# A weighted sum of 128 weight pieces moved from VectorE to TensorE's column tiles, and a norm's 1/rms moved behind the products

## The chip, the cores and the metric

One core of one Trainium2 chip runs the whole program. The metric is the device time of one execution in microseconds (us); lower is better. The engines are called as in the profile: PE (TensorE; PEld is its weight loading), DVE (VectorE), ACT (ScalarE), POOL (GpSimd) and SP, whose queue issues nearly all transfers.

## What is computed

Three blocks follow each other on 256 tokens of width 2048, all in float32.

1. The first block has two layers. Each layer is an RMS norm, one wide input projection, three kinds of attention (A with 6 heads, B with 6, C with 4), a gate on each head's output, and an output projection that is added to x:

```
h = _rms_norm(x, norm_g[l])
proj = jnp.einsum('bsd,dn->bsn', h, w_in[l])
a_out = a_out.reshape(Bsz, S, A_DIM) * jax.nn.silu(a_gate)
x = x + jnp.einsum('bsm,md->bsd', mixed, w_out[l])
```

2. The second block is one layer of banded attention, modulated by rows that are computed from a conditioning vector c: `silu(c) @ w_ada + b_ada`, eight rows of 2048 numbers (six for this and the next block, two for the final norm). They depend on nothing in the first block. The product is a matrix of 2048 x 16384 numbers with one vector, 128 MB that are read once.
3. The third block routes each token to two of 32 experts and reads all experts' weights.

`_rms_norm(x, g)` is `x * rsqrt(mean(x*x) + eps) * g`. The factor rsqrt(...) is one number for each token, so it commutes with a product over the features: (r x g) W = r ((x g) W).

## The kernel before

**Pieces.** The weights of the first and second block come in pieces of 128 x 2048 numbers, 1 MB each: 73 pieces for each layer of the first block and 52 for the second block. A piece of the kinds "tok" and "out" holds 4 tiles of 128 features by 512 columns and gives rows of tokens; a piece of the kind "feat" holds 16 tiles of 128 by 128 and gives rows of features. The product is made exact with three TensorE passes: ACT copies a piece into a rounded head (`split_head`, L736), DVE subtracts to get the tail (`split_tail`, L1141), and PE multiplies head by head, head by tail and tail by head (`three`, L925 to L927): 24 matmuls over 512 columns for a tok or out piece, 48 over 256 columns for a feat piece. ACT and DVE split two pieces ahead of PE (`AHEAD`); three split pieces fit at a time.

**The modulation pieces** (`w_ada`, 128 of them) share the ring of five 1 MB buffers (`raw`) with the weights. The stream alternates: weight piece g+2, then modulation piece a, and so on; 16 out of 18 weight pieces have one beside them (`ada_after`). DVE handles such a piece in the step "ada": the piece times one number of silu(c) for each partition, added to a sum of 128 x 2048 (L1217 for the first, L1221 for the other 15 of a row). After 16 pieces PE sums over the partitions with a matrix of ones in four matmuls with 32 stationary columns each (step "ada_sum", L1109), ACT copies the result, and PE transposes it (step "ada_turn", L1117).

**Order.** Every engine walks the same list of steps (`layer_schedule`): a piece, and behind it the steps due there ("score", "turn", "value", "gate", "subnorm", "ada", ...). "turn" is the transposition of the softmax's probabilities (L1085), "value" the product with the values (L1094, L1096), both for one head. Each engine runs its own part in that order, and semaphores connect them. The layer begins with a step "norm": ACT squares x, POOL takes the power -1/2 of the mean, DVE makes a diagonal matrix of 1/rms (L1166), PE multiplies all of x with it (transposed and scaled at once, 32 matmuls, L939), and ACT and DVE write the gained result and its head and tail. Only then does the first piece begin: it waits for the last tail.

**PSUM.** There are eight banks of 128 x 512. In the first block, products rotate over banks 0 to 3, scores use 4 and 5, "turn", "subnorm", "ada_sum" and "ada_turn" share 6, "value", "forget" and "cumsum" share 7 (`psum_plan`). A step that writes a bank first waits until the bank's last content has been read (`bank_for`). The second block has a plan of its own: both heads of a "turn" pair use bank 6, one after the other (L1805, read by ACT L1687).

**The third block** starts after the second. It reads 384 MB of expert weights through a ring of its own; its first transfers are issued when the block starts.

Of the kernel before, what the change touches and what calls it, by code (L numbers as in the profile page):

```python
# [27 lines left out]
P = 128  # L28
# [22 lines left out]
for _name, _n in (("norm_g", 16), ("qn_g", 4), ("kvn_g", 2), ("b_forget", 6), ("lam", 256),  # L51
                  ("subln_g", 1), ("lam_init", 1), ("one_minus", 1), ("w_f", 96)):
    PAR[_name] = (_at, _at + _n)
    _at += _n
# [3 lines left out]
class Tally:  # L58
# [6 lines left out]
    def add(self, sem, event):  # L65
        table = self.order.setdefault(sem, {})
        assert event not in table, (sem, event)
        table[event] = len(table) + 1

    def total(self, sem):  # L70
        return len(self.order.get(sem, {}))

    def at(self, sem, event, it=0, each=1):

        n = self.order[sem][event]
        if isinstance(it, int):
            return each * (it * self.total(sem) + n)
        return it * (each * self.total(sem)) + each * n

    def end(self, sem, it=0, each=1):  # L80
        n = self.total(sem)
        return each * (it + 1) * n if isinstance(it, int) else it * (each * n) + each * n
# [137 lines left out]
def first_parameters(norm_g, qn_g, kvn_g, b_forget, lams, subln_g, w_in):  # L220

    par = np.zeros((DEPTH + 1, P, N_PAR), np.float32)

    def put(name, l, a):
        par[l, :, PAR[name][0]:PAR[name][1]] = a
    for l in range(DEPTH):
# [4 lines left out]
        put("lam", l, np.concatenate([v[l] for v in lams])[None, :])  # L231
# [5 lines left out]
    return par  # L237
# [33 lines left out]
def layer_schedule():  # L271
# [12 lines left out]
    def followers(i, piece):  # L284
# [6 lines left out]
        if i == 0:  # L291
            out.append((i, ("forget",)))
        if i == 2:
# [23 lines left out]
        if piece[0] == "out" and piece[2] == 3:  # L317
            out.append((i + 1, ("squares", piece[1])))
# [20 lines left out]
    return [("norm",)] + steps  # L339


def psum_plan(steps, tally):
# [6 lines left out]
    def take(event, bank=None):  # L349
# [3 lines left out]
        where[event] = bank  # L353
        tally.add(f"full{bank}", event)
        tally.add(f"free{bank}", event)

    n_score = 0
    for s in steps:
        kind = s[0]
        if kind == "norm":  # L360
            for j in range(8):
                take(("norm", j))
# [48 lines left out]
ACT_LINKS_1 = 1  # L411
DVE_LINKS_1 = 71
# [12 lines left out]
def first_block(nc, whole, ctx, d, x, ssq_x, c0, mod):  # L425
    steps = layer_schedule()
    tally = Tally()
    bank_of = psum_plan(steps, tally)
# [9 lines left out]
    gate_no = {g: n for n, g in enumerate(gates)}  # L438

# [14 lines left out]
    for i in range(n_pieces):  # L454
        for part in range(2):
            tally.add("head_split", (i, part))
# [2141 lines left out]
```

## Time and profile before

| | |
|---|---|
| median of 3 runs | 2504.33 us (2497.93 to 2508.22) |
| profiled execution, its own time | 2505.9 us |
| its span | 2504.1 us, so 1.8 us lie around it |
| PE busy / PEld busy | 2264.2 us (90%) / 1680.4 us (67%) |
| DVE busy | 1413.3 us (56%); 282.4 us of it are the 120 instructions of L1221 |
| ACT busy | 727.6 us (29%) |
| HBM read | 757.28 MB, 304 GB/s over the span |
| first block / second / third | about 0 to 1063, 1063 to 1479, 1479 to 2504 us |

Busy time is the union of an engine's instructions. A matmul's record is longer than the step from one matmul to the next, since they are pipelined: steps are read from the differences of the start times. One float32 matmul (as in L1109, L939, L1094) leaves two records, so "x8" means four matmuls. The granted clock (PEclk) is given as a share of 2.4 GHz; 0.5 is 1.2 GHz.

### The profile page before, as it was taken

The numbers are of one execution on the slowest core, as the hardware profiler recorded it, in microseconds if no ns is written. First come the engines' busy times: TensorE is split into PE (matmuls) and PEld (weight loads), VectorE is DVE, ScalarE is ACT, GpSimd is POOL, SyncE is SP. The second block draws the span as 40 slices with busy tenths as digits, with TensorE's granted clock in tenths as the row PEclk, the third lists the DMA queues.
The fourth block names the chain that finished last, engine by engine and source line by source line (L and its number), as shares of the span: only waits on it lengthen the run. The fifth ranks groups of instructions, "written<-read, shape, count | busy, mean of one in ns | idle before, by whom it ended". The sixth has DMA issues, their size and how long they took to land. (4 is left out here: it accounts for less than half of the span.)

```text
span 2504.1 us, 37242 instructions
## 1 busy us (share of the span) xinstructions
PE 2264.2 (90%) x14757; PEld 1680.4 (67%) x14757; DVE 1413.3 (56%) x2015; ACT 727.6 (29%) x1347; POOL 40.7 (2%) x62
## 2 busy tenths in 40 slices
PE   6999999989999998979999987999888888888886
PEld 5889988778899997867788774454444444444442
DVE  3878799875787898855545535333333333333334
ACT  3443544442443544345545422000000000000001
POOL 0100000000000000030000000000000000000000
PEclk8999999998999999989999987999999999999998
DMA  5877767865877776774334434999999999999997
GB/s 215 330 305 291 276 236 269 305 270 215 348 263 291 262 262 255 290 261 141 132 126 138 143 143 185 421 422 422 422 422 422 422 422 422 422 422 422 422 422 312
DMA packets 108689, 761.83 MB, mean 304 GB/s; under 512 B 12288, under 2 KB 15520, under 8 KB 16800
## 3 DMA queue, kind: packets, MB, share of 16 engines
q1 hardware_dynamic: 108288, 759.30, 76.8%
q8 instruction: 76, 1.25, 0.2%
q10 hardware_dynamic: 288, 0.98, 0.1%
q14 instruction: 37, 0.30, 0.0%
HBM read 757.28 MB, written 2.95 MB: 304 GB/s over the span
## 5 line engine op out<-in xcount | busy, mean ns | idle before, releaser
L2263 PE MATMUL b_ps<-s_raw,s_window 128*64 128x256 f32 x4096 | 461.0, 382 | 58.7 <-DVE x_tokens L2489 39.3
L2263 PEld LDWEIGHTS b_ps<-s_raw,s_window 128*64 128x64 f32 x4096 | 295.3, 137 | 236.0 <-issue 72.6
L1141 DVE TENSOR_TENSOR s_w_tail<-s_raw,s_w_head 128x1024 fp32r<-128x1024 f32 x292 | 345.3, 1223 | 44.8 <-ACT s_w_head L736 44.7
L925 PE MATMUL b_ps<-s_h_head,s_w_head 128*128 128x256 f32 x1184 | 345.2, 292 | 0.0
L926 PE MATMUL b_ps<-s_h_tail,s_w_head 128*128 128x256 f32 x1184 | 337.9, 285 | 0.0
L927 PE MATMUL b_ps<-s_h_head,s_w_tail 128*128 128x256 f32 x1184 | 337.9, 285 | 0.0
L736 ACT ACTIVATE s_w_head<-s_raw 128x1024 fp32r<-128x1024 f32 x292 | 293.8, 1052 | 129.1 <-DMA s_raw<-in_w 76.4
L1221 DVE SCALAR_TENSOR_TENSOR s_ada_acc<-s_raw,s_c_col,s_ada_acc 128x2048 f32<-128x2048 f32 x120 | 282.4, 2354 | 0.0
L2283 PE MATMUL b_ps<-s_raw,s_diag 128*64 128x512 f32 x1024 | 238.3, 600 | 39.9 <-DMA s_raw<-in_w_down 24.6
L925 PEld LDWEIGHTS b_ps<-s_h_head,s_w_head 128*128 128x128 f32 x1184 | 230.1, 194 | 13.1 <-issue 11.0
L926 PEld LDWEIGHTS b_ps<-s_h_tail,s_w_head 128*128 128x128 f32 x1184 | 230.4, 195 | 0.2
L927 PEld LDWEIGHTS b_ps<-s_h_head,s_w_tail 128*128 128x128 f32 x1184 | 230.0, 194 | 0.0
L2171 ACT ACTIVATE s_hidden<-b_ps 128x256 f32<-128x256 f32 x32 | 12.3, 384 | 645.3 <-PE b_ps L2263 645.3
L2283 PEld LDWEIGHTS b_ps<-s_raw,s_diag 128*64 128x64 f32 x1024 | 65.9, 136 | 191.6 <-DMA s_raw<-in_w_down 84.1
L2481 DVE TENSOR_TENSOR s_y<-b_ps,s_gate_row 128x512 f32<-128x512 f32 x64 | 44.3, 692 | 238.3 <-PE b_ps L2283 238.3
L925 PE MATMUL b_ps<-s_w_head,s_h_head 128*128 128x512 f32 x416 | 168.1, 404 | 6.4 <-issue 6.4
L926 PE MATMUL b_ps<-s_w_tail,s_h_head 128*128 128x512 f32 x416 | 166.3, 400 | 0.0
L2489 DVE TENSOR_TENSOR x_tokens<-b_ps,x_tokens 128x1024 f32<-128x1024 f32 x128 | 147.8, 1217 | 32.5 <-PE b_ps L2298 32.5
L927 PE MATMUL b_ps<-s_w_head,s_h_tail 128*128 128x512 f32 x416 | 165.8, 399 | 0.0
L1840 DVE TENSOR_TENSOR s_w_tail<-s_raw,s_w_head 128x1024 fp32r<-128x1024 f32 x104 | 126.3, 1253 | 69.5 <-ACT s_w_head L1611 69.3
L1730 PE MATMUL b_ps<-s_h_head,s_w_head 128*128 128x256 f32 x416 | 121.0, 291 | 0.0
L1731 PE MATMUL b_ps<-s_h_tail,s_w_head 128*128 128x256 f32 x416 | 118.9, 286 | 0.0
(340 smaller groups left out, 3168.2 us busy)
## 6 DMA issues: line engine op xcount, KB each, us to landing
s_raw<-in_w SPq DMA_DIRECT2D x198, 1024.0 KB, 5.8
s_raw<-in_w_ada SPq DMA_DIRECT2D x128, 1024.0 KB, 5.1
s_raw<-in_w_gate SPq DMA_DIRECT2D x128, 1024.0 KB, 24.1
s_raw<-in_w_up SPq DMA_DIRECT2D x128, 1024.0 KB, 26.5
s_raw<-in_w_down SPq DMA_DIRECT2D x128, 1024.0 KB, 26.8
x_tokens<-in_x SPq DMA_DIRECT2D x1, 2048.0 KB, 7.7
s_rel<-in_rel SPq DMA_DIRECT2D x1, 2048.0 KB, 11.5
s_raw<-mod_rows SPq DMA_DIRECT2D x2, 1024.0 KB, 12.2
```

What stands on the lines that cost most here:

```text
L736: act.activation(w_head[:, g % SPLITS, cols], raw[:, ring, cols], ACT.Copy)\
L925: pe.matmul(out, head, m_head, start=first, stop=False, skip_group_check=True)
L926: pe.matmul(out, head, m_tail, start=False, stop=False, skip_group_check=True)
L927: return pe.matmul(out, tail, m_head, start=False, stop=last, skip_group_check=True)
L1141: dve.tensor_tensor(w_tail[:, g % SPLITS, cols], raw[:, slot["w", g], cols], w_head[:, g % SPLITS, cols].bitcast(F32), ALU.subtract)\
L1221: ins = dve.scalar_tensor_tensor(out=ada_acc[:, :], in0=raw[:, ring, :], scalar=c_col[:, 2, k:k + 1], in1=ada_acc[:, :], op0=ALU.mult, op1 ...
L1730: pe.matmul(out, head, m_head, start=first, stop=False, skip_group_check=True)
L1731: pe.matmul(out, head, m_tail, start=False, stop=False, skip_group_check=True)
L1840: dve.tensor_tensor(w_tail[:, i % SPLITS, cols], raw[:, i % RAW, cols], w_head[:, i % SPLITS, cols].bitcast(F32), ALU.subtract)\
L2263: ins = pe.matmul(psum[64 * h:64 * h + 64, c // 4, 0:T], window[:, 4 * (c % 4) + k, :], raw[:, c, k * 512 + h * T:k * 512 + h * T + T], st ...
L2283: ins = pe.matmul(psum[rows_n, 4 + n % 2, :], hidden_t[:, m_ % 2, 64 * (m_ // 2):64 * (m_ // 2) + 64], raw[:, 8 + m_, n * 512:(n + 1) * 51 ...
L2489: dve.tensor_tensor(xs, psum[:, bank:bank + 2, :], xs, ALU.add).then_inc(sem["x_added"], 1)
```

## The change

- Each modulation piece is multiplied and summed by PE: four matmuls with 32 equal stationary columns (the piece's column of silu(c), repeated), one for each 512 columns of the piece, written to four groups of 32 partitions of bank 7, and accumulated there over 16 pieces (L1149 in the changed kernel). The steps "ada" on DVE and "ada_sum" on PE are gone; ACT copies the bank instead.
- x is transposed without 1/rms (L967, `turn_x`), and its head and tail are made of x times the gain. The transposition of the next layer's x is spread between the last pieces of the layer and the first pieces of the next. 1/rms is applied to the outputs: as ACT's scale for tok pieces, as a DVE product with a row `rrow` for q, k and gates. DVE, not ACT, now reads q, k and gate outputs from PSUM. The gate's sigmoid is three ACT instructions (Exp, Ln, Exp) instead of one on ACT and a reciprocal on DVE.
- Bank plan of the first block: "value", "forget" and "cumsum" move from bank 7 to bank 6. "forget" and "cumsum" come 4 pieces later. Parameters of both layers are loaded at the start.
- Second block: the second head of each "turn" pair gets bank 3, and the feat pieces' banks are assigned anew.

```diff
@@ all_steps, new
+NEXT_NORM = {("out", 1, 3): [("squares", 0), ("turn_x", 0)],
+             ("out", 2, 0): [("squares", 1), ("turn_x", 1), ("split_x", 0)],
+             ("out", 2, 1): [("split_x", 1)],
+             ("out", 3, 0): [("squares", 2), ("turn_x", 2)],
+             ("out", 3, 2): [("split_x", 2)],
+             ("out", 3, 3): [("split_x", 3)]}
+
+THIS_NORM = {("tok", 0, 0): [("squares", 3), ("turn_x", 3)],
+             ("tok", 0, 1): [("split_x", 4)],
+             ("tok", 0, 2): [("x_rows",)]}
...
@@ psum_plan
-        elif kind in ("turn", "subnorm", "ada_sum", "ada_turn"):
+        elif kind == "ada" and s[1] % 16 == 0:
+            take(("ada_sum", s[1] // 16), 7)
+        elif kind in ("turn", "subnorm", "ada_turn"):
             take(s, 6)
         elif kind in ("value", "forget", "cumsum"):
-            take(s, 7)
+            take(s, 6)
...
@@ TensorE
+                if kind == "turn_x":
...
+                                ins = pe.transpose(ps[:, col:col + P], x_tiles[:, t, 4 * n + 2 * j + k, :], ident)
...
-                        if what == "tok" and g == 0:
-                            pe.wait_ge(sem["h_tail"], at("h_tail", 7, l))
+                        if what == "tok" and n == 0:
+                            pe.wait_ge(sem["h_tail"], at("h_tail", (0, 2, 3, 4)[g], l))
...
-                elif kind == "ada_sum":
-
-                    pe.wait_ge(sem["ada_done"], at("ada_done", 16 * s[1] + 15, l))
-                    ps = bank_for(pe, s, l)
+                elif kind == "ada":
+
+                    i = s[1]
+                    j, k = i // 16, i % 16
+                    piece = ("ada", l * ADA_PIECES + i)
+                    ring = slot[piece]
+                    ev = ("ada_sum", j)
+                    ps = bank_for(pe, ev, l) if k == 0 else psum[bank_of[ev, l]]
...
+                    pe.wait_ge(sem[f"raw{ring}"], at(f"raw{ring}", piece, 0, 16))
                     for g in range(4):
-                        ins = pe.matmul(ps[32 * g:32 * g + 32, :], ones[:, 0:32], ada_acc[:, 512 * g:512 * g + 512],
-                                        start=True, stop=True, skip_group_check=True)
-                    ins.then_inc(sem[f"full{bank_of[s]}"], 1)
+                        ins = pe.matmul(ps[32 * g:32 * g + 32, :], repeated_column(c_col[:, 2, k:k + 1], 32),
+                                        raw[:, ring, 512 * g:512 * g + 512], start=k == 0, stop=k == 15,
+                                        skip_group_check=True)
+                    ins.then_inc(sem["ada_done"], 1)
...
@@ VectorE
+                    if what == "feat" and s[3] in ("aq", "ak", "cq", "ck", "kr"):
...
+                            dve.tensor_tensor(out, ps[:, 0:T], rrow[:, :], ALU.mult).then_inc(free_sem(ev, l), 1)
...
-                    chain.link(dve.tensor_scalar(gate[:, g, :], gate[:, g, :], 1.0, None, ALU.add))
-                    chain.link(dve.reciprocal(gate[:, g, :], gate[:, g, :]))
                     dve.tensor_tensor(gate[:, g, :], gate[:, g, :], gate_raw[:, :], ALU.mult)\
                        .then_inc(sem["gate"], 1)
-                elif kind == "ada":
...
-                        ins = dve.scalar_tensor_tensor(out=ada_acc[:, :], in0=raw[:, ring, :],
-                                                       scalar=c_col[:, 2, k:k + 1], in1=ada_acc[:, :],
-                                                       op0=ALU.mult, op1=ALU.add)
-                    ins.then_inc(sem["ada_done"], 1)
...
@@ second_attention
-                take(s[2:], 2 + feats % 2)
+                take(s[2:], {"ka": 2 + feats % 2, "qa": 2, "qb": 0, "kb": 2}[s[3]])
...
-        elif kind in ("turn", "onorm"):
+        elif kind == "turn":
+            take(s, 3 if s[3] else 6)
+        elif kind == "onorm":
             take(s, 6)
```

Three places show how the order on PE moves. The first is the step behind a key piece of attention A, in the first layer (L1072 and L1077 are the score, L1105 and L1110 in the changed kernel; `s_raw` is the ring with the modulation piece). Before:

```order
L925 MATMUL b_ps<-s_h_head,s_w_head 128x256
L926 MATMUL b_ps<-s_h_tail,s_w_head 128x256
L927 MATMUL b_ps<-s_h_head,s_w_tail 128x256
L1072 MATMUL b_ps<-s_qk 128x128 [waits b1_free7,b1_free3,b1_free2]
L1077 MATMUL b_ps<-s_ncum,c_sb 128x128
```

and changed:

```order
L949 MATMUL b_ps<-s_h_head,s_w_head 128x256
L950 MATMUL b_ps<-s_h_tail,s_w_head 128x256
L951 MATMUL b_ps<-s_h_head,s_w_tail 128x256
L1149 MATMUL b_ps<-s_raw,s_c_col 32x512 [waits b1_raw1]
L1149 MATMUL b_ps<-s_raw,s_c_col 32x512 x3
L1105 MATMUL b_ps<-s_qk 128x128 [waits b1_free6,b1_free5,b1_free3,b1_free2]
L1110 MATMUL b_ps<-s_ncum,c_sb 128x128
```

The four matmuls of a modulation piece now stand between the piece and the score that reads its output. In the whole list there are 128 such groups; 47 of them have pieces on both sides, 81 have at least one other small step (a score, a turn, a value, a transposition) beside them.

The second place is attention B of the first layer, where the value of one head is followed at once by the turn of the next. Before (L1094 and L1096 are the value, L1085 the turn):

```order
L1094 MATMUL b_ps<-s_p_t,s_v_ab 128x256 [waits b1_free7,b1_free1,b1_free6]
L1096 MATMUL b_ps<-s_p_t,s_v_ab 128x128
L1085 MATMUL b_ps<-c_sb,s_s_buf 128x128 [waits b1_free6,b1_probs]
L1085 MATMUL b_ps<-c_sb,s_s_buf 128x128 x2
L1072 MATMUL b_ps<-s_nope_k,s_mixed 128x128 [waits b1_free4,b1_roped,b1_free1]
```

and changed:

```order
L1129 MATMUL b_ps<-s_p_t,s_v_ab 128x128
L1118 MATMUL b_ps<-c_sb,s_s_buf 128x128 [waits b1_free6,b1_probs]
L1118 MATMUL b_ps<-c_sb,s_s_buf 128x128 x2
L1149 MATMUL b_ps<-s_raw,s_c_col 32x512 [waits b1_raw1]
L1149 MATMUL b_ps<-s_raw,s_c_col 32x512 x3
L1105 MATMUL b_ps<-s_nope_k,s_mixed 128x128 [waits b1_free4,b1_roped,b1_free1]
```

The order of value and turn is the same, but both now write bank 6, so the turn's wait on `b1_free6` is now a wait for DVE to read the value just computed; before, bank 6 last held the previous turn. This pair occurs five times in a layer.

The third place is the end of the first layer. Before, L939 is the norm's product, of which the first 20 of 32 matmuls stand here; the second layer's first piece follows the last of them and waits for `b1_h_tail`:

```order
L926 MATMUL b_ps<-s_w_tail,s_h_head 128x512
L927 MATMUL b_ps<-s_w_head,s_h_tail 128x512
L939 MATMUL b_ps<-s_diag,x_tokens 128x128 [waits b1_diag,b1_free3,b1_free2]
L939 MATMUL b_ps<-s_diag,x_tokens 128x128 x15
L939 MATMUL b_ps<-s_diag,x_tokens 128x128 [waits b1_free0]
L939 MATMUL b_ps<-s_diag,x_tokens 128x128 x3
```

and changed, after the piece ("tok", 0, 0) of the second layer:

```order
L967 MATMUL b_ps<-c_sb,x_tokens 128x128 [waits b1_free4,b1_free3,b1_free2]
L967 MATMUL b_ps<-c_sb,x_tokens 128x128 x3
L967 MATMUL b_ps<-c_sb,x_tokens 128x128 [waits b1_free5]
L967 MATMUL b_ps<-c_sb,x_tokens 128x128 x3
L1149 MATMUL b_ps<-s_raw,s_c_col 32x512 [waits b1_raw0,b1_free7]
L1149 MATMUL b_ps<-s_raw,s_c_col 32x512 x3
L949 MATMUL b_ps<-s_w_head,s_h_head 128x512 [waits b1_h_tail,b1_tail_split]
```

The 32 products in one lump have become four groups of 8 transpositions between pieces, the last of them behind the next layer's first piece.

## Rows read from the trace of the kernel before

**Rows 1.** Windows: us, busy PE, PEld, DVE, ACT, POOL, PEclk, DMA share, GB/s

```profile
200.00:400.00 200.00, 196.84 (x1500) 184.22 (x1499) 174.69 (x249) 87.64 (x168) 0.00 (x0) 0.99 0.74 274
494.00:520.00 26.00, 26.00 (x117) 21.44 (x116) 25.65 (x20) 12.59 (x19) 0.00 (x0) 1.00 1.01 419
1560.00:2504.00 944.00, 826.16 (x5636) 408.38 (x5632) 322.95 (x390) 44.40 (x111) 2.30 (x4) 0.99 1.00 415
```

**Rows 2.** The chain that ended last, in the third block: start, us, what

```profile
2172.05 27.76 DMA s_raw<-in_w_up
```

**Rows 3.** Waits of PE, 0 to 1030 us: us in total, times, longest

```profile
PE b_ps L925 <- DVE s_h_tail L1341: 6.4, 2, 3.2
...
PE b_ps L1109 <- DVE s_ada_acc L1221: 5.8, 2, 2.9
PE b_ps L1072 <- issue: 5.7, 10, 0.6
```

**Rows 4.** Timeline of PE around one ada_sum: start, us, engine, instruction

```profile
680.28 0.28 PE L927 MATMUL b_ps<-s_h_head,s_w_tail 128*128 128x256 f32 x1
680.49 1.06 PE L1109 MATMUL b_ps<-s_ada_acc,c_sb 128*32 128x512 f32 x8
681.49 0.38 PE L925 MATMUL b_ps<-s_h_head,s_w_head 128*128 128x256 f32 x1
681.71 0.28 PE L926 MATMUL b_ps<-s_h_tail,s_w_head 128*128 128x256 f32 x1
```

**Rows 5.** Timeline of PE, an ada_sum right behind a value

```profile
285.80 1.07 PE L1109 MATMUL b_ps<-s_ada_acc,c_sb 128*32 128x512 f32 x8
286.80 0.38 PE L925 MATMUL b_ps<-s_low_head,s_w_head 128*128 128x256 f32 x1
```

**Rows 6.** A group of DVE's, page part 5: busy, mean ns, idle before

```profile
L1221 DVE SCALAR_TENSOR_TENSOR s_ada_acc<-s_raw,s_c_col,s_ada_acc 128x2048 f32<-128x2048 f32 x120 | 282.4, 2354 | 0.0
```

**Rows 7.** Timeline of PE between the layers

```profile
543.78 0.39 PE L927 MATMUL b_ps<-s_w_head,s_h_tail 128*128 128x512 f32 x1
548.83 10.13 PE L939 MATMUL b_ps<-s_diag,x_tokens 128*128 128x128 f32 x64 [4.67 <-DVE s_diag L1166]
562.14 0.77 PE L925 MATMUL b_ps<-s_w_head,s_h_head 128*128 128x512 f32 x1 [3.18 <-issue]
...
568.50 0.39 PE L925 MATMUL b_ps<-s_w_head,s_h_head 128*128 128x512 f32 x1
```

**Rows 8.** Timelines of PE and DVE, a value and a turn in attention B

```profile
341.84 0.38 PE L1096 MATMUL b_ps<-s_p_t,s_v_ab 128*128 128x128 f32 x2
342.06 0.49 PE L1085 MATMUL b_ps<-c_sb,s_s_buf 128*128 128x128 f32 x3
342.39 0.39 PE L1072 MATMUL b_ps<-s_nope_k,s_mixed 128*128 128x128 f32 x2
...
343.64 0.42 DVE L1325 TENSOR_TENSOR s_mixed<-b_ps,s_gate 128x256 f32<-128x256 f32 x1
```

**Rows 9.** Timeline of PE at the start of the program

```profile
23.42 10.02 PE L939 MATMUL b_ps<-s_diag,x_tokens 128*128 128x128 f32 x64 [6.42 <-DVE s_diag L1166]
36.62 0.77 PE L925 MATMUL b_ps<-s_w_head,s_h_head 128*128 128x512 f32 x1 [3.18 <-issue]
```

**Rows 10.** Timeline of PE, piece and score in attention A

```profile
226.44 0.28 PE L927 MATMUL b_ps<-s_h_head,s_w_tail 128*128 128x256 f32 x1
227.30 0.46 PE L1072 MATMUL b_ps<-s_qk 128*128 128x128 f32 x2 [0.58 <-issue]
```

**Rows 11.** Second block: timelines of PE and DVE at a turn

```profile
1163.90 0.49 PE L1805 MATMUL b_ps<-c_sb,s_s_buf 128*128 128x128 f32 x3
1165.62 0.52 PE L1805 MATMUL b_ps<-c_sb,s_s_buf 128*128 128x128 f32 x3 [1.23 <-ACT s_p_t L1687]
...
1163.84 0.35 DVE L1931 TENSOR_SCALAR s_s_buf<-s_s_buf,s_stat 128x256 f32<-128x256 f32 x1
```

**Rows 12.** Instructions of L1109: duration min/median/max in ns, first and last start

```profile
L1109 PE MATMUL b_ps<-s_ada_acc,c_sb x64: 592/617/926, 154.9 to 1055.9; 128*32 128x512 f32 x64
```

More of the change, by code:

```diff
@@ L63, in __init__, with add @@
         self.order = {}
-    def add(self, sem, event):
+    def add(self, sem, event, it=0):
         table = self.order.setdefault(sem, {})
[L67 to L71, printed above, removed]
+        assert (event, it) not in table, (sem, event, it)
+        table[event, it] = len(table) + 1
     def at(self, sem, event, it=0, each=1):
[L75 to L82, printed above, removed]
+        return each * self.order[sem][event, it]
 class Chain:
@@ L352, in take @@
             turn[0] += 1
-        where[event] = bank
-        tally.add(f"full{bank}", event)
-        tally.add(f"free{bank}", event)
+        where[event, l] = bank
+        tally.add(f"full{bank}", event, l)
+        tally.add(f"free{bank}", event, l)
     n_score = 0
-    for s in steps:
+    for l, s in flat:
         kind = s[0]
-        if kind == "norm":
-            for j in range(8):
-                take(("norm", j))
+        if kind == "turn_x":
+            for j in range(2):
+                take(("turn_x", s[1], j), 4 + j)
+        elif kind == "x_rows":
+            take(s, 6)
         elif kind == "piece":
@@ L627, in x_done, with tile_ready, gate_slot, before @@
             freed(eng, ("out", 3, t), l)
+    def tile_ready(eng, j, l):
+        for bank in range(2):
+            freed(eng, ("turn_x", SPLIT_TILES[j][0] // 4, bank), l)
+        if l:
+            last = {0: ("feat", "cg", 3), 1: ("feat", "cg", 3), 2: ("out", 3, 1), 3: ("out", 3, 2), 4: ("out", 3, 3)}[j]
+            piece_used(eng, piece_at[last], l - 1)
+    def gate_slot(g, l):
+        return (l * len(gates) + gate_no[g]) % 3
+    def before(events, n, l):
+        return (events[n], l) if n >= 0 else (events[n + len(events)], l - 1)
     def gate_used(eng, g, l):
@@ L1271, in _ @@
                     sl = a % 2
-                    if a >= 2:
-                        full(dve, ("turn",) + scores[a - 2][1:3], l)
+                    if a >= 2 or l:
+                        last, l_last = before(scores, a - 2, l)
+                        full(dve, ("turn",) + last[1:3], l_last)
                     bias = {"A": fox_mask, "B": chunk_mask, "C": c_bias[:, h % 4, :]}[name]
@@ L1808, in _ @@
                 _, name, t = s
-                freed(pe, ("turn", name, t, 1))
+                for j in range(2):
+                    freed(pe, ("turn", name, t, j))
                 if t == 0:
```

579 lines of the change are left out of this document (304 added, 275 removed).

## The prediction

> **What bounds the kernel now.** I read the windows first, then the chain of waits, PE's waits, and the timelines of PE at the places that the change touches. The windows show two regimes. In the first block PE is busy 196.8 of 200 us, and through the output pieces 26.00 of 26 us, with 117 matmuls of 0.222 us each, while DVE is busy 87% and 99% of those stretches and DMA moves up to 419 GB/s [rows 1]. The reader is to see that a very busy DVE is not what PE waits for: PE's waits of the whole first block name DVE for 6.4 and 5.8 us [rows 3]. The third block moves 415 GB/s over 944 us, and its chain is one landing after the other [rows 1, 2]; its first transfer is issued at its start. So every microsecond that PE gains or loses in the first two blocks moves the third block by as much, and nothing there gives it back. The sum is one over PE's time, and idle DVE is worth nothing by itself.
>
> **The change part by part.**
>
> *The groups of four column tiles, added.* The operation exists in the trace: an ada_sum is four float32 matmuls with 32 stationary and 512 moving columns, one for each group of 32 output partitions. That is the shape of the new group, though its operands differ. From its start to the next matmul's start it takes 1.00 us [rows 4, 5]. Between pieces it costs more: from 680.28 to 681.71 there are 1.43 us, of which the two ordinary steps take 2 x 0.12 = 0.24, so 1.19 us [rows 4]. The other 0.19 us are the changes into and out of the group. The Trainium skill (TensorEngine Tiling (Array Packing), Key Properties) says that changing the tiling mode drains the engine, which speaks against a change that does it 256 times. By that rule the 0.19 belongs to every group that stands alone; without it they would cost 1.00 too, 9 us less in the sum. The row agrees with the rule here. Behind a float32 step such as a value, the price is 1.00 [rows 5]. The order has 47 groups alone and 81 beside a small step: 47 x 1.19 + 81 x 1.00 = 56 + 81 = **+137 us**. Nothing covers them: PE is full. Bounds: 128 x 1.00 = 128 and 128 x 1.19 = 152.
>
> *The eight ada_sum, removed,* with the same prices: 8 x 1.1 = **-9**. PE's wait for the last of the 16 sums, 5.8 us in two of them, goes too [rows 3]: **-5.8**. The next thing that PE needs there is a raw piece, issued early enough (below).
>
> *120 + 8 instructions of DVE, removed.* The 120 take 282.4 us [rows 6]. They lie beside PE's work. Priced at nothing, apart from waits counted in other lines.
>
> *The norm between the layers.* From 544.0 (543.78 and one step) to 562.14 is 18.1 us without a piece; then 15 steps take 6.36 us instead of 15 x 0.222 = 3.3, at 1.2 GHz, the lower of the two clock levels, after the idle gaps and small products: 3.0 [rows 7]. That is 21.1 gone, since the first tiles are ready pieces ahead and the last have two pieces of time. Added are 32 transpositions; a turn has three in 0.33 us [rows 8], so 32 x 0.11 = 3.5. **-17.6**. Each group of transpositions waits for an addition to x that is a piece old, and for two copies on ACT and DVE, also with a piece between.
>
> *The start.* The first piece starts at 36.62, behind 10.02 us of product and 3.18 us of waiting for the last tail, all after a wait of 6.42 us [rows 9]. Now 24 transpositions stand there, and only the first four of 16 tiles must be ready, but ACT still does its squares, copies and heads in one line, and PE still transposes 12 tiles before the piece. Bounds 0 and -13 (23.42 to 36.62). I take **-7**, the middle.
>
> *The row of 1/rms:* two float32 products a layer. At that level one of the norm's takes 10.13 / 32 = 0.32 us [rows 7]; with the change of mode 2 x (0.64 + 0.19), **+1.6**. Its wait for POOL has two pieces of time.
>
> *Score A.* Today PE stands from 226.44 to 227.30, 0.86 us where a step is 0.12, ten times, since ACT must first read the key [rows 3, 10]. Now a group of 1.0 us lies in between, and DVE's read of 0.42 us goes on beneath it. 10 x 0.74 = **-7.4**; 0 if DVE comes late.
>
> *Value and turn in one bank, attention B.* Today the turn starts at 342.06, 0.22 us after the value's second half [rows 8]. Now DVE must have read the value. At best it reads at once: 342.22 + 0.42 = 342.64, 0.6 us late. At worst it comes as late as today: 343.64 + 0.42 = 344.06, 2.0 us late [rows 8]. DVE loses a sum of 2.35 us [rows 6] and a reciprocal, but gains a wait for ACT's three-step sigmoid. I take 1.3, ten times: **+13** (6 to 20). Queued behind the turn are the group, the score and the next piece.
>
> *The h_tail wait before the last third of an output piece,* 6.4 us [rows 3]: its chain over ACT and DVE stays. **-1** (0 to -6.4).
>
> *Second block.* The second turn starts 1.72 us after the first, though the three transpositions take 0.27 and DVE's probabilities are ready at 1163.84 + 0.35 = 1164.19 [rows 11]. With a bank of its own it can start at about 1164.2: 1.4 us, 16 times, **-22** (at least the idle time, 16 x 1.23 = 19.7). The copies on ACT are then needed one piece later, by the value.
>
> *Moved at no cost:* q, k and gates read by DVE instead of ACT, forget and cumsum four pieces later, parameters loaded early. Cover: DVE sheds 2.35 us per group and takes on about 1.5 us per feat piece. Without that cover each late read would stall a piece.
>
> *SP's queue.* A modulation piece's buffer is now freed by PE behind its piece, about one piece later. The ring has five buffers; the piece that takes this one is needed by ACT more than two pieces later. PE's time for a piece and a group grows from 24 x 0.222 = 5.3 to 6.4 us for the same 2 MB: 328 GB/s where 419 flow today without a wait of PE [rows 1]. Priced at nothing.
>
> Sum: 137 - 9 - 5.8 - 17.6 - 7 + 1.6 - 7.4 + 13 - 1 - 22 = **+82 us**. The profiled execution took 2505.9 us (span 2504.1), 1.6 above the median of 2504.3; on the median, 2504.3 + 82 = **2586 us**. Without the groups everything else is -55 us, so the change breaks even at 55 / 128 = 0.43 us a group.
>
> **The rivals.**
>
> *The groups cost less, to a point below break-even (faster).* All eight ada_sum stand alone; none is one of a stream that accumulates in a bank. If the loads slipped ahead and the four tiles ran as one pass at the price of an ordinary 512-column step, 0.22 us [rows 1], 128 groups would cost 28 us: 2504 + 28 - 55 = 2477. It decides from 0.43 us down. Against it: eight records in 1.06 us, the same alone and behind a value [rows 4, 5]. 5%.
>
> *The group spans one record.* A record of L1109 lasts 617 ns [rows 12]. If the four tiles start together and both passes fit into that, a group costs 0.62 + 0.19 = 0.81 us, 104 us in all, so 2504 + 104 - 55 = 2553. The Trainium skill (TensorE: Matmul & The Clock Gate, Measured speedup vs the span model) gives this rule: one matmul's duration and about 4 ns for each further tile. Against it, again, the 1.06 us of the row, which fits two such passes in turn. 8%.
>
> *PE waits for modulation pieces.* PE now stands in line for each landing. If SP's queue, blocked on a buffer that PE frees, made each of the 64 or so groups in tok and out stretches wait 1 us, it would be 2586 + 64 = 2650. For it: the 1.01 share of DMA today [rows 1]. Against it: five buffers and slower consumption. 8%.
>
> *DVE becomes the one that is late.* In B it has a wait on ACT inside the gate, and now stands between PE and every q, k and gate. 0.4 us for each of the 74 feat pieces is +30, 2616. 7%.
>
> **How the numbers follow.** The forecast, 2586, has 70%. Its own bounds: all groups at 1.00 (-9), the pair in B at 0.6 (-7), the start at -13 (-6), the h_tail wait gone (-5): 2559. All groups at 1.19 (+15), B at 2.0 (+7), start 0 (+7), score A not covered (+7): 2622. The rival at 2553 and clock dips that may vanish pull the lower end to 2545, the late DVE the upper to 2628; what is left out is the first rival, the third and the tails, some 20%. A measurement of this kernel can tell about 0.5%, 12.5 us, from no change. Faster by more: 6%, the first rival and a little. Within it, 2492 to 2517: 5%. Slower: 89%.
>
> **What would show it.** PE's new line: 512 float32 matmuls, eight records in about 1.06 us, and 137 us by start-to-start. DVE's busy time down by some 270 us or more with no gain from it. Between the layers no gap over 1 us and no drop of the clock; the first piece at about 30 us. In B a wait of PE's turn on DVE's read of the value, about 1.3 us ten times. In the second block no wait of L1805's successor for ACT. The third block as long as before, only later. Wrong: a group that takes well under 0.8 us, or PE waits of more than 20 us in total on `in_w_ada` landings or on DVE's q and k reads.

## The result, and the profile after

The changed kernel takes 2579.95 us (median of 4 runs, 2575.81 to 2587.35) where the kernel before takes 2504.97 us beside it: a ratio of 1.030 [1.028, 1.032], slower by 75 us. The forecast was 2586, its range 2545 to 2628. The profiled execution took 2587.35 us, 7.4 above that median; its span is 2585.6, so 81.5 us more than the span before.

The head of the page of the kernel after:

```profile
span 2585.6 us, 38908 instructions
...
PE 2382.7 (92%) x15661; PEld 1683.2 (65%) x15661; DVE 1117.9 (43%) x1923; ACT 738.8 (29%) x1345; POOL 41.3 (2%) x61
...
PEclk9899999999999999998999997999999999999998
...
DMA 26%; PE 10%; DVE 2%; issue 1%; ACT 1%; SPq 0%; POOL 0%; POOLq 0%; DVEq 0%; ACTq 0%
...
L1149 PE MATMUL b_ps<-s_raw,s_c_col 128*32 128x512 f32 x1024 | 136.6, 605 | 0.0
```

DVE's busy time fell from 1413.3 to 1117.9 us, by 295, and the kernel is slower all the same. PE has one new line, L1149, of 1024 records: 128 groups of four matmuls of two records each. It is never idle ahead of a group, so the groups' time comes on top.

Where the 81.5 us lie is read from two milestones on PE's timeline: the transposition of mod, which ends the first block, and the first product with x_tokens behind the second one. Two kernels stand here; before:

```profile
1069.92 0.30 PE L1734 MATMUL b_ps<-c_sb,mod 128*128 128x128 f32 x1 [1.79 <-PEq L2592]
...
1482.64 1.65 PE L2198 MATMUL b_ps<-s_diag,x_tokens 128*128 128x128 f32 x6 [5.79 <-DVE s_diag L2315]
```

and after:

```profile
1169.95 0.30 PE L1784 MATMUL b_ps<-c_sb,mod 128*128 128x128 f32 x1 [1.79 <-PEq L2644]
...
1562.26 6.01 PE L2249 MATMUL b_ps<-s_diag,x_tokens 128*128 128x128 f32 x27 [5.78 <-DVE s_diag L2366]
```

The first block is 1169.95 - 1069.92 = 100.0 us longer. The second takes 392.3 where it took 412.7, 20.4 less. From there to the end it is 1023.3 for 1021.5, 1.9 more. The prediction's terms for these three were +103.8, -22 and 0.

PE's waits of the first block, after; they answer to [rows 3] and to the start of [rows 9]:

```profile
PE b_ps L942 <- DMA s_c_col<-in_c_col: 12.9, 1, 12.9
PE b_ps L1118 <- DVE s_mixed L1372: 10.7, 10, 2.9
PE b_ps L967 <- ACT s_mixed L801: 4.7, 2, 3.2
PE b_ps L967 <- DVE s_nope_k L1166: 2.0, 1, 2.0
PE b_ps L1158 <- ACT s_o_c L918: 1.3, 2, 0.7
```

Three waits have gone: those for h_tail, for ada_acc and before A's scores. No modulation piece is waited for. One line is new, L1118: the turn in B waits until DVE has read the value out of the same bank. (L967 is the transposition of x at the start.) The timeline has one such place (value, turn, next group):

```profile
359.90 0.38 PE L1129 MATMUL b_ps<-s_p_t,s_v_ab 128*128 128x128 f32 x2
360.90 0.52 PE L1118 MATMUL b_ps<-c_sb,s_s_buf 128*128 128x128 f32 x3 [0.61 <-DVE s_mixed L1372]
361.35 1.06 PE L1149 MATMUL b_ps<-s_raw,s_c_col 128*32 128x512 f32 x8
```

Here the turn starts 1.00 us behind the value's second half, where it was 0.22 [rows 8]. The next rows show a group between two steps of a tok piece and a group ahead of a score of A, then the window between the layers, all of the kernel after:

```profile
104.14 0.39 PE L951 MATMUL b_ps<-s_w_head,s_h_tail 128*128 128x512 f32 x1
104.46 1.06 PE L1149 MATMUL b_ps<-s_raw,s_c_col 128*32 128x512 f32 x8
105.46 0.50 PE L949 MATMUL b_ps<-s_w_head,s_h_head 128*128 128x512 f32 x1
105.79 0.39 PE L950 MATMUL b_ps<-s_w_tail,s_h_head 128*128 128x512 f32 x1
...
244.42 1.06 PE L1149 MATMUL b_ps<-s_raw,s_c_col 128*32 128x512 f32 x8
245.41 0.49 PE L1105 MATMUL b_ps<-s_qk 128*128 128x128 f32 x2
```

```profile
560.00:600.00 40.00, 40.00 (x194) 29.52 (x194) 18.47 (x21) 17.32 (x22) 0.00 (x0) 1.00 0.76 273
```

From 104.14 to 105.79 there are 1.65 us, of which the two ordinary steps take 0.45. So the group costs 1.20 us: 1.00 from its own start to the next start, and about 0.10 on either side, since the step before it and the step behind it are longer than usual. Behind a small float32 step the price is the same. A turn and the piece behind it, before:

```profile
214.09 0.49 PE L1085 MATMUL b_ps<-c_sb,s_s_buf 128*128 128x128 f32 x3
...
214.53 0.28 PE L926 MATMUL b_ps<-s_h_tail,s_w_head 128*128 128x256 f32 x1
```

and a turn, a group and a piece, after:

```profile
229.46 0.49 PE L1118 MATMUL b_ps<-c_sb,s_s_buf 128*128 128x128 f32 x3
229.88 1.06 PE L1149 MATMUL b_ps<-s_raw,s_c_col 128*32 128x512 f32 x8
...
231.10 0.28 PE L950 MATMUL b_ps<-s_h_tail,s_w_head 128*128 128x256 f32 x1
```

0.44 us have become 1.64, again 1.20 more. By the starts in the trace, 120 of the 128 groups cost 1.19 us and 8 between 0.88 and 1.0: about 150 us in all. Counted from each group's own start to the next start alone, they are 127.5 us.

The score starts with the group's end, without a gap. The window between the layers, after, is full at a granted clock of 1.00 (2.4 GHz): the gap of 18 us [rows 7] is gone, and the slow steps behind it.

### The profile page after: what moved, and what is told of

The parts are those of the page before. It is cut to its first block and busy times, and to the rows that moved or that the text cites. A ratio compares the mean times of both kernels' runs of the same rounds, so it can differ in the third digit from the quotient of the medians.

```text
span 2585.6 us, 38908 instructions
## 1 busy us (share of the span) xinstructions
PE 2382.7 (92%) x15661; PEld 1683.2 (65%) x15661; DVE 1117.9 (43%) x1923; ACT 738.8 (29%) x1345; POOL 41.3 (2%) x61
## 5 line engine op out<-in xcount | busy, mean ns | idle before, releaser
L950 PE MATMUL b_ps<-s_h_tail,s_w_head 128*128 128x256 f32 x1184 | 335.9, 284 | 0.0
L1149 PE MATMUL b_ps<-s_raw,s_c_col 128*32 128x512 f32 x1024 | 136.6, 605 | 0.0
L2349 PE MATMUL b_ps<-s_y,s_weigh_t 64*128 64x512 f32 x512 | 118.5, 602 | 0.0
```

Of the source, the lines that this page charges most:

```text
L950: pe.matmul(out, head, m_tail, start=False, stop=False, skip_group_check=True)
L1149: ins = pe.matmul(ps[32 * g:32 * g + 32, :], repeated_column(c_col[:, 2, k:k + 1], 32), raw[:, ring, 512 * g:512 * g + 512], start=k == 0, ...
L2349: ins = pe.matmul(psum[:, PART_BANKS[t][n], :], weigh_t[rows_n, t * P:(t + 1) * P], y[rows_n, n % 2, :], start=True, stop=True)
```

## Experiments

Each run is given as its ratio to the kernel before on the same chip, whose median was 2506.97 us for the first four, 2500.66 for the next four, 2502.96 for the three after those and 2504.66 for the last. "Below" and "above the change" are differences to its median of 2579.95, which comes from another chip; by the ratios these differences come out 2 to 4 us elsewhere.

**The modulation back on DVE, all else as changed.**

```diff
-                        ins = pe.matmul(ps[32 * g:32 * g + 32, :], repeated_column(c_col[:, 2, k:k + 1], 32),
-                                        raw[:, ring, 512 * g:512 * g + 512], start=k == 0, stop=k == 15,
+                        ins = pe.matmul(ps[32 * g:32 * g + 32, :], ones[:, 0:32], ada_acc[:, 512 * g:512 * g + 512],
...
+                        ins = dve.scalar_tensor_tensor(out=ada_acc[:, :], in0=raw[:, ring, :],
+                                                       scalar=c_col[:, 2, k:k + 1], in1=ada_acc[:, :],
+                                                       op0=ALU.mult, op1=ALU.add)
```

> The changed kernel with one part undone: the modulation pieces are multiplied on VectorE and summed by four TensorE products per 16 pieces as before, and value, forget and cumsum are back in bank 7; the norm's new order and the second block's banks stay. If the groups on TensorE are what costs (the theory), this is the better kernel of the three: from 2505, -20 for the second block, -6 for the start, -18 for the norm between the layers, +2 for the row, and up to +7 because VectorE, full again, reads q and k late: about 2463, faster than before by 1.6%. If VectorE's load was what held the first block (the rival), most of the loss should stay: about 2560 to 2600.

Measured: 2470.71 us, 0.987 [0.985, 0.988]. (Value, forget and cumsum stand in bank 7 again, the sums in 6.) The expectation had 2463. So the rest of the change, without the groups, is a gain of 36 us (the prediction's terms for what this kernel keeps make -46: the norm, the start, the row, h_tail and the second block), and the move to TensorE costs 109 us against it, 111 by the ratios. The first block ends at 1057.49, 12.4 earlier than before and 112.5 earlier than with the groups. Part of the price of DVE's modulation is seen too:

```profile
PE b_ps L1102 <- issue: 19.0, 16, 3.1
...
PE b_ps L946 <- DVE s_h_tail L1395: 6.8, 2, 3.5
```

Score gaps had 5.7 us at 10 places before [rows 3]. With q and k read by DVE, behind modulation work, they are 19.0 at 16: the ten before A's scores are as long as before, 0.56 us each, and 13.4 us stand at six places before C's. The changed kernel has neither line. The groups thus hide, and relieve, some 26 us that DVE's modulation would cost here.

**B's values in rotating banks.**

```diff
+        elif kind == "value" and s[1] == "B":
+            take(s)
```

> The changed kernel with the values of attention B in the rotating banks 0 to 3 instead of bank 6, which they share with the turn. The theory says that the turn's wait on VectorE's read of the value goes: ten idle times of 0.6 to 2.9 us, each some 0.2 us longer by start to start, so -12 to -14 us against the changed kernel, about 2567. The rival is that something else then becomes late at the same place (the probabilities, or the bank of a feat piece): 2575 to 2580.

Measured: 2567.16 us, 1.024 [1.023, 1.026], 12.8 below the change. By the ratios it is 15 below. The wait of L1118 is gone and no other takes its place. The first block ends at 1153.7, 16.3 earlier, which is more than the wait: the clock gains too (shown under "Why the prediction was right"). The term of +13 for the shared bank is shown, or a little more.

**The second block's banks alone, on the kernel before.**

```diff
-                take(s[2:], 2 + feats % 2)
+                take(s[2:], {"ka": 2 + feats % 2, "qa": 2, "qb": 0, "kb": 2}[s[3]])
-        elif kind in ("turn", "onorm"):
+        elif kind == "turn":
+            take(s, 3 if s[3] else 6)
-                freed(pe, ("turn", name, t, 1))
+                for j in range(2):
+                    freed(pe, ("turn", name, t, j))
```

> The kernel before with the second block's banks of the changed kernel and nothing else. Theory: 16 second turns start 1.3 to 1.4 us earlier, so -20 to -22 us: 2484. Rival: the gain in the changed kernel's second block had another cause (what the first block leaves behind), then it stays at 2505.

Measured: 2486.05 us, 0.991 [0.988, 0.993], 20.9 us less. Of PE's waits of the second block before, the first line is the one that goes:

```profile
PE b_ps L1805 <- ACT s_p_t L1687: 19.1, 16, 2.2
PE b_ps L1744 <- DVE s_diag L1861: 12.7, 1, 12.7
```

**Groups of half the columns.**

```diff
+                        w = 512 if k == 0 else 256
-                        ins = pe.matmul(ps[32 * g:32 * g + 32, :], repeated_column(c_col[:, 2, k:k + 1], 32),
-                                        raw[:, ring, 512 * g:512 * g + 512], start=k == 0, stop=k == 15,
+                        ins = pe.matmul(ps[32 * g:32 * g + 32, 0:w], repeated_column(c_col[:, 2, k:k + 1], 32),
+                                        raw[:, ring, 512 * g:512 * g + w], start=k == 0, stop=k == 15,
```

> The changed kernel in which 120 of the 128 groups multiply only 256 of each tile's 512 columns, so half of the modulation's products are left out. Which part of a group sets its 1.00 us? If it is the columns that stream by, four tiles at once (theory), a group takes about 0.55 us and the kernel 120 x 0.45 = 54 us less: 2526. If it is the eight weight loads of some 106 ns each, one after the other (rival), a group stays at 0.85 us or more and the kernel gains at most 18 us: 2562 or more.

Measured: 2535.44 us, 1.011 [1.010, 1.013], 44.5 below the change. One group and the step behind it:

```profile
103.62 0.64 PE L1150 MATMUL b_ps<-s_raw,s_c_col 128*32 128x256 f32 x8
104.19 0.50 PE L949 MATMUL b_ps<-s_w_head,s_h_head 128*128 128x512 f32 x1
```

0.57 us for 1.00, with the same 32-column weight loads. So 256 columns are worth 0.43 us, and within the 1.00 the part that depends on no column is 1.00 - 2 x 0.43 = 0.14. The 120 groups should give 52 us less: the first block ends 49.7 earlier (1120.3), and the medians are 44.5 apart.

**DVE's modulation thinned, on the kernel before.**

```diff
-                        ins = dve.scalar_tensor_tensor(out=ada_acc[:, :], in0=raw[:, ring, :],
-                                                       scalar=c_col[:, 2, k:k + 1], in1=ada_acc[:, :],
+                        ins = dve.scalar_tensor_tensor(out=ada_acc[:, 0:256], in0=raw[:, ring, 0:256],
+                                                       scalar=c_col[:, 2, k:k + 1], in1=ada_acc[:, 0:256],
```

> The kernel before, with DVE's multiply and add of each modulation piece behind the first of a set of sixteen cut to 256 of the 2048 columns (it leaves out seven eighths of those products; TensorE's work is untouched). About 112 x 2.0 us = 224 us of DVE work go, nearly as much as the change took from it. Theory (DVE's work lay beside TensorE's): only the waits on late DVE results go, those for ada_acc (5.8 us), for h_tail (6.4 us) and for the score's late reads (5.7 us): 2507 goes to some 2490. Rival (DVE's busy time is what the first block waits for, and the change lost only because it gave TensorE the same work back): 60 us and more go, 2445 or below.

Measured: 2485.90 us, 0.994 [0.993, 0.996]; 14.8 us less. The page's group of that line:

```profile
L1221 DVE SCALAR_TENSOR_TENSOR s_ada_acc<-s_raw,s_c_col,s_ada_acc 128x256 f32<-128x256 f32 x120 | 57.3, 478 | 0.0
```

282.4 us [rows 6] became 57.3: 225 us of DVE work are worth 15. They are the waits for late results: the lines of ada_acc (5.8), of h_tail behind DVE (6.4) and of the turn behind s_buf (1.7) are gone from the list, 13.9 in all. The score gaps of 5.7 stay, which the expectation had counted in: ACT reads q and k there, not DVE. This run says what relieving DVE could be worth in the kernel before.

**All four matmuls of a group in one column tile.**

```diff
-                        ins = pe.matmul(ps[32 * g:32 * g + 32, :], repeated_column(c_col[:, 2, k:k + 1], 32),
+                        at_row = 0 if k else 32 * g
+                        ins = pe.matmul(ps[at_row:at_row + 32, :], repeated_column(c_col[:, 2, k:k + 1], 32),
```

> The change, with the four matmuls of every group but the first of a set written to the same 32 rows, so that all four stand in one column tile (the sums come out elsewhere and mixed; same count, columns and weight loads). Theory (four column tiles run beside each other, and a group costs about one record of 512 columns and some switching): 112 groups go from 1.00 us to four records one after the other, between 2.5 (four of 0.62) and 3.4 us (four of 0.85, twice the 0.43 us that 256 columns cost less): +168 to +270 us, about 2840. Rival (the groups' price is set by the weight loads and by what surrounds them, and the tiles share nothing): the price stays near 1.0 us, and the time within 2580 to 2600.

Measured: 2891.98 us, 1.156 [1.155, 1.158]; 312 above the change. A group and the step behind it:

```profile
101.20 3.62 PE L1150 MATMUL b_ps<-s_raw,s_c_col 128*32 128x512 f32 x8
104.75 0.50 PE L949 MATMUL b_ps<-s_w_head,s_h_head 128*128 128x512 f32 x1
```

3.55 us for 1.00: 2.55 more, times the 120 groups behind a set's first (the expectation said 112, which was a slip) is 306, and the first block is 307 us longer (1477.3). The tiles do run beside each other. Each further matmul in the same tile adds 2.55 / 3 = 0.85 us, the value that the half columns give too (2 x 0.43). That is the whole of one float32 matmul of 512 columns, and almost four of the ordinary steps of 0.222 [rows 1].

**Groups in bf16.**

```diff
-                        ins = pe.matmul(ps[32 * g:32 * g + 32, :], repeated_column(c_col[:, 2, k:k + 1], 32),
-                                        raw[:, ring, 512 * g:512 * g + 512], start=k == 0, stop=k == 15,
+                        upper = c_col[:, 2, k:k + 1].bitcast(BF16)[:, 1:2]
+                        ins = pe.matmul(ps[32 * g:32 * g + 32, :], repeated_column(upper, 32),
+                                        raw[:, ring, 512 * g:512 * g + 512].bitcast(BF16)[:, 1::2], start=k == 0, stop=k == 15,
```

> The change, with both operands of the groups' matmuls read as the upper halves of their values (bf16, the rest of each value is left out of the modulation's products; same count of matmuls, columns and bytes between them). Theory (a group's price is its columns times the passes that its type needs): a group of four 512-column tiles costs about 0.21 us for the columns (the 256-column fp32r record is followed by the next 0.12 us later) and some 0.15 to 0.2 us of switching, 0.4 us in place of 1.00: 120 x 0.6 = 72 us less, 2580 goes to some 2508, which is level with before. Rival (loads and switching, about half of the price whatever the type): 120 x 0.4 us or less go, 2532 or above.

Measured: 2506.67 us, 1.0023 [1.0010, 1.0036], 73 below the change (70 by the ratios): within 0.3% of before, as expected. A group now has four records:

```profile
106.00 0.39 PE L952 MATMUL b_ps<-s_w_head,s_h_tail 128*128 128x512 f32 x1
106.33 0.41 PE L1151 MATMUL b_ps<-s_raw,s_c_col 128*32 128x512 bf16 x4
106.66 0.50 PE L950 MATMUL b_ps<-s_w_head,s_h_head 128*128 128x512 f32 x1
107.00 0.39 PE L951 MATMUL b_ps<-s_w_tail,s_h_head 128*128 128x512 f32 x1
```

From its start to the next start a group takes 0.34 us for 1.00 (0.338 unrounded). Over all 128 groups these times add up to 46.4 us for 127.5, so 81.0 less, and the first block is 80.4 shorter (1089.58): what the groups give arrives. In ten of them the wait of A's score for DVE's read of k is no longer covered (0.63 us in place of 0.34), which is the line of 2.3 us before A's scores that is back in PE's list.

The prediction's break-even of 0.43 counts the whole price, with the longer steps around a group. In that measure the bf16 group costs 107.00 - 106.00 - 0.45 = 0.55 us, above 0.43, and the time is 6.0 us over that of before. So break-even lies at 0.55 - 6.0 / 128 = 0.50. Two other kernels give 0.77 - 28.5 / 128 = 0.55 (half the columns) and 1.19 - 75 / 128 = 0.60 (the change) in the same way. It is 0.5 to 0.6 us, somewhat above the 0.43.

**Five tries to go below the first run.** It is the fastest kernel of this study, so its 19.0 us before the scores were worth a try. Each edit below is made to the first run's kernel. First, scores of A and C one piece later, with A's turn and value:

```diff
-            out += [(i, ("score", "A", h, 0)), (i + 1, ("turn", "A", h)), (i + 2, ("value", "A", h))]
+            out += [(i + 1, ("score", "A", h, 0)), (i + 2, ("turn", "A", h)), (i + 3, ("value", "A", h))]
-            out += [(i, ("score", "C", h, 0)), (i, ("score", "C", h, 1)), (i + 2, ("turn", "C", h)),
+            out += [(i + 1, ("score", "C", h, 0)), (i + 1, ("score", "C", h, 1)), (i + 2, ("turn", "C", h)),
```

> The change with the modulation back on DVE (2470.7 us), and the scores of attention A and C one piece later in the order (A's turn and value too), so that TensorE has a piece of its own to do while DVE gets to the read of k behind its modulation work. Theory (with the modulation on DVE the price is paid in late reads, 19.0 us at 16 places before a score): those 19 us go and some of the small gaps before the other scores, 2470 goes to about 2450. Rival (the lateness only moves to the turn or the value behind the score): 2465 to 2475.

Measured: 2473.17 us, 0.989 [0.988, 0.991]. The 19.0 are gone, and these stand in PE's list in their place:

```profile
PE b_ps L946 <- DVE s_h_tail L1395: 10.2, 2, 5.1
PE b_ps L1139 <- ACT s_p_t L911: 6.6, 2, 3.3
PE b_ps L1115 <- DVE s_s_buf L1359: 5.1, 2, 2.7
...
PE b_ps L1139 <- DVE s_ada_acc L1272: 4.6, 2, 2.7
```

The rival has it: the lateness moves. Next, DVE's modulation step last at its place in the order:

```diff
+        out.sort(key=lambda e: e[1][0] == "ada")
```

> The change with the modulation back on DVE (0.9867 of before), and DVE's modulation step put behind the score's, the softmax's and the gate's work of the same place in the order. Theory (the modulation step of 2.3 us stands in DVE's queue ahead of work that TensorE waits for): the score's, turn's and h_tail's waits (19.0 + 2.2 + 6.8 us) fall by a third or so, 5 to 12 us, 0.983 of before. Rival (what delays DVE's reads is the step of the piece ahead, wherever in it that step stands): no change, 0.986 to 0.988.

Measured: 2485.15 us, 0.993 [0.991, 0.994], worse. The waits before scores grow to 24.0 us, and in the window from 300 to 600 the granted clock falls from 0.97 to 0.95. The window of the first run, then that of this one:

```profile
300.00:600.00 300.00, 287.42 (x1738) 253.01 (x1737) 243.23 (x359) 135.72 (x235) 3.01 (x5) 0.97 0.72 272
```

```profile
300.00:600.00 300.00, 287.68 (x1734) 254.41 (x1733) 237.85 (x354) 136.63 (x238) 3.01 (x5) 0.95 0.70 267
```

PE is as busy in both, but its products run slower. The first block ends 13.5 us later (1071.0), while the waits of PE's list grow by less than 4. Third, C's scores one piece later, with turn, value and sub-norm:

```diff
-            out += [(i, ("score", "C", h, 0)), (i, ("score", "C", h, 1)), (i + 2, ("turn", "C", h)),
-                    (i + 3, ("value", "C", h)), (i + 4, ("subnorm", h))]
+            out += [(i + 1, ("score", "C", h, 0)), (i + 1, ("score", "C", h, 1)), (i + 3, ("turn", "C", h)),
+                    (i + 4, ("value", "C", h)), (i + 5, ("subnorm", h))]
```

> The change with the modulation back on DVE, and attention C's two scores one piece later with its turn, value and sub-norm a piece later too; attention A stays. Theory (6 of the 16 waits before a score, with 13.4 of the 19.0 us, stand before C's scores; moving A's as well, and C's turn not, took the gain back): those 13 us go, 0.981 to 0.983 of before. Rival (they return at the turn or at the end of the layer, where the last sub-norm comes later): 0.986 or above.

Measured: 2475.10 us, 0.988 [0.986, 0.990]. The score line fell to 5.6 us as expected, and PE's list has these instead:

```profile
PE b_ps L946 <- DVE s_h_tail L1395: 10.2, 2, 5.2
PE b_ps L1139 <- DVE s_ada_acc L1272: 7.5, 2, 3.9
PE b_ps L1115 <- ACT s_o_c L915: 6.2, 2, 3.2
```

Both edits together:

> Both edits together, DVE's modulation step last at its place and attention C a piece later. If both gains stand and are separate: 0.976 to 0.980 of before, about 2450 us; if either returns elsewhere, as the better of the two alone.

Measured: 2480.07 us, 0.990 [0.988, 0.992], between the two. Last, only the step at C's q pieces, behind the read of k:

```diff
+            at = i + 1 if piece[:2] == ("feat", "cq") else i
-            out.append((i, ("ada", a)))
+            out.append((at, ("ada", a)))
...
-                out += [(i + 1, ("ada_sum", a // 16)), (i + 2, ("ada_turn", a // 16))]
+                out += [(at + 1, ("ada_sum", a // 16)), (at + 2, ("ada_turn", a // 16))]
```

> The change with the modulation back on DVE (0.9867 of before), and the DVE modulation step that stands at each of attention C's q pieces put one place later, behind DVE's read of k; nothing else moves, the order of the transfers included. In the timeline DVE reads k at 372.39 where TensorE was done with it at 369.9, and the step at q (367.86, 2.34 us) stands right ahead. Theory (a DVE queue that is 2.3 us shorter ahead of the read of k takes 2.3 us off each wait before a score of C): of the 13.4 us at 6 places 9 to 12 go, 0.982 to 0.984 of before. Rival (as in the three orders before: what goes here comes back at the turn, the value or h_tail, and in the clock): 0.986 to 0.989.

Measured: 2478.50 us, 0.990 [0.988, 0.992]. The first score of C shows that the mechanism is real and that it is local. The first run, then this one:

```profile
372.90 1.02 PE L1102 MATMUL b_ps<-s_qk 64*128 64x128 f32 x8 [2.94 <-issue]
395.51 1.74 PE L1102 MATMUL b_ps<-s_qk 64*128 64x128 f32 x8 [3.14 <-issue]
```

```profile
369.22 1.01 PE L1103 MATMUL b_ps<-s_qk 64*128 64x128 f32 x8 [0.69 <-issue]
392.03 1.02 PE L1103 MATMUL b_ps<-s_qk 64*128 64x128 f32 x8 [3.13 <-issue]
```

The first gap of each layer fell by 2.25 us, about the length of the step moved (2.34); the second here did not, and the third grew from 1.44 to 2.46. All 16 gaps together fell from 19.0 to 17.2 us, where 9 to 12 had been expected, and the wait for h_tail grew from 6.8 to 9.7. In C a shift of DVE's queue is paid a few pieces later. DVE has little slack there: between 350 and 376 us of the first run it pauses only for two waits of 1.6 us on ACT's sigmoid and one of 0.3. None of the five orders came below 2470.7, though the intervals of the two best, 0.989 and 0.988, overlap with the first run's. Less DVE work would be another way, which no run here tries. None of these runs settles how much of the 109 us between the first run and the change would come back if C alone used the groups.

## Why the prediction was right

The mechanism was right: the groups' time comes on top of a full TensorE, and relieving DVE gives almost nothing back. The sum, +82, met +81.5 in the profiled spans and +75 in the medians. That it fits so closely is partly luck, since the groups cost 13 us more than forecast and other terms about as much less. By its own steps:

- **What bounds it.** "Idle DVE is worth nothing by itself" holds: 225 us of DVE's work alone are worth 15 (DVE's modulation thinned), of which 12.2 are the two waits that [rows 3] count by name. The third block kept its length within 2 us.
- **The groups, +137, were the term most off:** about 150, at its own upper bound of 152. The 1.19 for a group between pieces was right. The 1.00 for the 81 beside a small step was not: [rows 5] were counted from the ada_sum's own start, which leaves out the longer steps on both sides of it. Turn, group and piece take 1.20 us more than turn and piece, like a group that stands alone. The Trainium skill (TensorEngine Tiling (Array Packing), Key Properties) says that a change of tiling mode drains the engine. The traces agree in kind: the steps around a group are 0.20 us longer at nearly every one of the 128. No run separates a drain from other costs of the switch.
- **The rival of one record, 0.81 us, fell.** Its rule is the span model of the Trainium skill (TensorE: Matmul & The Clock Gate, Measured speedup vs the span model). The traces agree with it if its unit is the whole float32 matmul with both of its records: four tiles took 1.00 us where each further matmul in one tile adds 0.85. One record of 0.6 was the wrong unit.
- **ada_sum -9, its wait -5.8.** The lines are gone; the wait's 5.8 went in the thinned run as well.
- **The norm between the layers, -17.6, and the start, -7.** Both happened as described. The first piece starts at 30.68 for 36.62, 5.9 earlier, and only its first three steps are slow (the fourth, at 32.07, has 0.23 us to the next), where 15 were. With those 2.7 the start gave nearly 9.
- **Score A, -7.4.** Covered: the score starts at the group's end, and the ten gaps gave about 8.
- **Value and turn in one bank, +13.** Shown at 12.8, 15 by the ratios.
- **The h_tail wait, -1, was also mis-sized:** its 6.4 us went entirely. The copy and the subtraction of the last tiles now stand in a DVE queue without the 2.35 us step; the first and the fifth run bear that out, since the wait is 6.8 with the modulation on DVE and gone without its bulk.
- **The second block, -22.** -20.4 in the profile, -20.9 alone.
- **Moved at no cost, and the break-even of 0.43.** The reads of q, k and gates went to DVE at no cost because the groups take DVE's modulation away and stand ahead of A's scores. Without the groups that cover is gone: 19.0 us before the scores and 6.8 at h_tail, and the rest gives 36 us where its terms make 46. The forecast of the changed kernel is not touched by it. The break-even came out at 0.5 to 0.6 us a group.

With the groups at 150, the terms of the first block as measured add up to about 108 where it grew by 100.0. These 8 us of further gain are assigned to no line, but for the 1.7 of a wait for s_buf that went as well and was in no term.

The wait of the turn in B, where it is longest (2.9 us), also costs clock. The place and its window in the changed kernel:

```profile
406.43 0.52 PE L1118 MATMUL b_ps<-c_sb,s_s_buf 128*128 128x128 f32 x3 [2.92 <-DVE s_mixed L1372]
...
400.00:420.00 20.00, 17.08 (x125) 14.18 (x125) 10.62 (x26) 6.86 (x12) 0.00 (x0) 0.91 0.53 187
```

and the same window with B's values in rotating banks, where the wait is gone:

```profile
400.00:420.00 20.00, 20.00 (x163) 16.84 (x163) 12.78 (x33) 8.75 (x18) 0.00 (x0) 1.00 0.67 247
```

The granted clock is 1.00 for 0.91 there, and 1.00 for 0.94 at the same place of the second layer (960 to 980).

## What to carry to other kernels

Before work is moved off a busy engine, take most of it away without putting it anywhere and time that: here 225 us of DVE were worth 15, and the new home charged some 150. Column tiles share time, but a float32 group takes at least a whole float32 matmul: count almost four ordinary steps of 512 columns, and 0.3 us around them. Read the price of an inserted step from the step before it to the second one behind it, with and without it, and not from its own start. When a change bundles edits, time it with the doubtful part undone: here the rest alone was the best kernel, 1.3% below before.

## What had not been expected of the hardware

The price of a group has a part for its columns and type and a part that does not change. From its start to the next start, 512 columns took 1.00 us in float32 and 256 took 0.57; 512 in bf16 took 0.34. Less 0.86 for the columns in float32, and less an ordinary step of 0.22 in bf16, 0.14 and 0.12 are left. The longer steps on both sides add 0.20 in every one of these kernels. So about 0.3 us of a group are paid whatever it multiplies, over half of the bf16 group's 0.55.

The weight loads of 32 columns, eight in each float32 group and 105 to 110 ns long, do not set the price: with half the columns the same eight loads stood in 0.57 us, where one after the other they would take 0.85.

A lower clock can cost more than the waits that are seen. Over 300 to 600 us PE was busy 287.4 us in one order of DVE's steps and 287.7 in another, at a granted clock of 0.97 and 0.95. The second kernel is 0.6% slower, and its first block is 13.5 us longer with less than 4 us more of waiting.
